# Three small experts of a mixture layer run in the third, fifth and seventh place instead of the second, fourth and sixth

## The reference, cut to what matters

```python
def moe_swiglu(h, w_router, w_gate, w_up, w_down):
    logits = (h @ w_router).astype(jnp.float32)
    top_vals, top_idx = lax.top_k(logits, TOP_K)
    top_w = jax.nn.softmax(top_vals, axis=-1)
    combine = jnp.sum(jax.nn.one_hot(top_idx, N_EXPERTS) * top_w[..., None], axis=-2)
    y = jnp.zeros_like(h)
    for e in range(N_EXPERTS):
        y = y + combine[..., e:e + 1] * swiglu(h, w_gate[e], w_up[e], w_down[e])
    return y
```

## Time and profile before

| | us |
|---|---|
| median of 3 runs | 1440.68 (1440.64 to 1440.73) |
| the profiled execution, own time | 1441.36 |
| its span, first to last instruction | 1439.6 |

### The profile page before, as it was taken

One profiled execution on the slowest core, in us unless ns is written; L12 is line 12 of the kernel. 1 busy time (PEld: TensorE's weight loads), 2 busy tenths in 40 slices (PEclk: granted clock), 3 DMA queues, 4 the chain that ended last, 5 costly groups with the idle time before them and its releaser, 6 DMA issues.

```text
span 1439.6 us, 17466 instructions
## 1 busy us (share of the span) xinstructions
PE 1421.6 (99%) x6728; PEld 1154.7 (80%) x6728; DVE 1169.4 (81%) x1050; ACT 989.4 (69%) x991; POOL 55.4 (4%) x61
## 2 busy tenths in 40 slices
PE   9999999999999999999999999999999999999997
PEld 8977888888887788887778887778887778888885
DVE  5777755556677769889999889999889999899896
ACT  6566553434565668778887778887778877777774
POOL 1000000000000009200000000000000000002000
PEclk9999999999999999999999999999999999999999
DMA  9933655546653369999999999999999999999991
GB/s 350 376 102 120 203 179 201 183 140 197 200 173 125 127 236 370 422 396 371 422 421 421 422 420 393 421 422 420 422 421 395 418 422 421 421 397 375 421 382 56
DMA packets 96489, 460.08 MB, mean 320 GB/s; under 512 B 7656, under 2 KB 13304, under 8 KB 53392
## 3 DMA queue, kind: packets, MB, share of 16 engines
q1 hardware_dynamic: 91632, 444.63, 78.8%
q10 hardware_dynamic: 3312, 9.46, 1.8%
q0 software_dynamic: 1456, 4.79, 0.9%
HBM read 447.85 MB, written 11.01 MB: 319 GB/s over the span
## 4 chain that ended last, share of the span: by engine, by line
PE 83%; DVE 8%; ACT 4%; issue 3%; DMA 2%; SPq 0%; ACTq 0%; DVEq 0%
PE A L498 15%; PE A L500 15%; PE A L499 15%; PE DN L498 5%; PE DN L500 5%; PE DN L499 5%; DVE wlo L472 4%; PE A L504 3%; PE A L505 3%; PE DN L2016 2%; ACT whi L465 2%; DVE wlo_more L472 1%; DMA raw_more<-in_moe_w_down 1%; PE T L2030 1%; PE DN L504 1%
## 5 line engine op out<-in xcount | busy, mean ns | idle before, releaser
L472 DVE TENSOR_TENSOR wlo<-raw,whi 128x2048 fp32r<-128x2048 f32 (+1 forms) x252 | 563.8, 2251 | 124.2 <-ACT whi L465 123.6
L465 ACT ACTIVATE whi<-raw 128x2048 fp32r<-128x2048 f32 (+1 forms) x252 | 472.0, 1885 | 158.9 <-PE A L500 83.3
L472 DVE TENSOR_TENSOR wlo<-raw_more,whi 128x2048 fp32r<-128x2048 f32 x74 | 168.2, 2288 | 11.1 <-ACT whi L465 10.8
L498 PE MATMUL A<-whi,hTh 128*128 128x512 f32 (+2 forms) x448 | 174.4, 389 | 0.8 <-DVE wlo L472 0.7
L499 PE MATMUL A<-wlo,hTh 128*128 128x512 f32 (+2 forms) x448 | 169.9, 379 | 0.0
L500 PE MATMUL A<-whi,hTl 128*128 128x512 f32 (+2 forms) x448 | 169.8, 379 | 0.0
L498 PE MATMUL A<-whi,heTh 128*128 128x512 f32 x420 | 166.5, 396 | 0.0
L500 PE MATMUL A<-whi,heTl 128*128 128x512 f32 x420 | 163.9, 390 | 0.0
L499 PE MATMUL A<-wlo,heTh 128*128 128x512 f32 x420 | 163.6, 390 | 0.0
L465 ACT ACTIVATE whi<-raw_more 128x2048 fp32r<-128x2048 f32 x74 | 140.6, 1916 | 23.1 <-PE A L500 9.6
L472 DVE TENSOR_TENSOR wlo_more<-raw,whi_more 128x2048 fp32r<-128x2048 f32 x57 | 130.4, 2287 | 19.2 <-ACT whi_more L465 19.2
(11 more groups left out here) (367 smaller groups left out, 2314.4 us busy)
## 6 DMA issues: line engine op xcount, KB each, us to landing
raw<-in_moe_w_up SPq DMA_DIRECT2D x79, 1024.0 KB, 11.3
raw<-in_moe_w_down SPq DMA_DIRECT2D x78, 1024.0 KB, 12.7
raw<-in_moe_w_gate SPq DMA_DIRECT2D x77, 1024.0 KB, 12.9
raw_more<-in_moe_w_gate SPq DMA_DIRECT2D x35, 1024.0 KB, 13.5
raw_more<-in_moe_w_down SPq DMA_DIRECT2D x34, 1024.0 KB, 13.5
raw_more<-in_moe_w_up SPq DMA_DIRECT2D x33, 1024.0 KB, 12.5
raw<-in_w_in SPq DMA_DIRECT2D x22, 1024.0 KB, 6.8
raw<-in_dense_w_down SPq DMA_DIRECT2D x11, 1024.0 KB, 4.9
```

Of the source, the lines that this page charges most:

```text
L465: nc.scalar.activation(split_slot(u, e)[0][:, :n], raw_of(u, e)[:, :n], ACT.Copy).then_inc(hi_done, 1)
L472: nc.vector.tensor_tensor(lo[:, :n], raw_of(u, e)[:, :n], hi[:, :n].bitcast(F32), ALU.subtract).then_inc(lo_done, 1)
L498: nc.tensor.matmul(o, hi, wh, start=start, stop=False)
```

## The change

The tuple of small places becomes (2, 4, 6), counted from 0, and the arithmetic that turns an expert's rank by size into its place is adapted: the places are now computed counted from one (1, 2, 4, 6, 8 for the large, 3, 5, 7 for the small), and one is taken off where the scratch rows are computed.

```diff
-SMALL_AT = (1, 3, 5)
+SMALL_AT = (2, 4, 6)
...
+            turns_from_one = cst[:, K_IOTA + 1:K_IOTA + 1 + NE]
...
-            done(nc.vector.scalar_tensor_tensor(turn_raw[:], small[:], -4.5, place_of[:], ALU.mult, ALU.add))
+            done(nc.vector.scalar_tensor_tensor(turn_raw[:], small[:], -3.5, place_of[:], ALU.mult, ALU.add))
...
-            done(nc.vector.tensor_scalar(turn[:], turn_raw[:], 2.0, NE - 1.0, ALU.mult, ALU.min))
+            done(nc.vector.tensor_scalar(turn[:], turn_raw[:], 2.0, 1.0, ALU.mult, ALU.max))
...
-            done(nc.vector.tensor_scalar(turn_row[:], turn[:], float(P), None, ALU.mult))
+            done(nc.vector.tensor_scalar(turn_row[:], turn[:], -1.0, float(P), ALU.add, ALU.mult))
...
-            done(nc.vector.tensor_scalar(is_last[:], turn[:], NE - 1.5, None, ALU.is_gt))
-            done(nc.vector.tensor_scalar(not_last[:], turn[:], NE - 1.5, None, ALU.is_lt))
+            done(nc.vector.tensor_scalar(is_last[:], turn[:], NE - 0.5, None, ALU.is_gt))
+            done(nc.vector.tensor_scalar(not_last[:], turn[:], NE - 0.5, None, ALU.is_lt))
             done(nc.vector.tensor_tensor(taken[:], turn[:].unsqueeze(1).broadcast_to([P, NE, NE]),
-                                         turns.unsqueeze(2).broadcast_to([P, NE, NE]), ALU.is_equal))
+                                         turns_from_one.unsqueeze(2).broadcast_to([P, NE, NE]), ALU.is_equal))
```

## The result

| | before | after |
|---|---|---|
| median of 20 runs, us | 1440.76 (1440.60 to 1442.40) | 1442.83 (1442.15 to 1444.92) |
| ratio to before, 95% interval | | 1.0015 (1.0008 to 1.0021) |
| profiled span, us | 1439.6 | 1442.7 |

The changed kernel is 2.07 us slower: inside the range of 1439.9 to 1446.0 and inside the 0.2% called no change, but three times the 0.7 us of the forecast. The profiled run's own time was 1444.51 us, 1.68 above the median, so its span shows 3.1 us where the medians show 2.1: 0.1 before the experts begin, 0.56 in the first seven places, 2.22 in the eighth up to its last unit and 0.3 behind that.

What follows compares the result with a forecast made beforehand. PE was taken to set the places' times, with DMA also near its limit. Terms 0 + 0 + 0.7 + 0 + 0 = +0.7 us, added to the median 1440.68, gave 1441.4 us, range 1439.9 to 1446.0.

Steps and rivals of the forecast that it cites:

- What bounds the places: All places: PE sets the large ones, PE with DVE the small; PE's 4.6 us of waits bound any gain.
- three signs of being wrong: PE waiting over 3 us in the eighth place, the seventh over 100 us, or a small place below 98 us.
- The boundaries (term 0): First seven places: same large-small boundaries in both orders, so their sum stays unchanged to about 0.1 us.
- The stall at the end of a small place (term 0): Last small place: its extra 0.53 us, read as emptied buffers, stays in the seventh; -0.5 if it goes.
- `weigh_last` (term 0): DVE, seventh place: 1.2 us of work moves into a small place, hidden by 1.45 us of idling; otherwise 1.2.
- The eighth place (term +0.7): Eighth place's start: without stock, gains and gathers cost loads 6.2 us; cushions of 1.4 and 4.1 leave 0.7.
- the step on SP's queue: Eighth place's loads, seven buffers: cost 0, hidden by what is in flight; without that cover 2 to 3 us more.
- the cushion at unit 14: Large place with empty start: DVE finished unit 14 at 1224.27, PE began it at 1228.40, 4.1 us in hand.
- The turns between the DMA queues: Gathers beside loads: equal turns would end the gathers in 10 us, term about 1 us; trace said not to show it.
- The starved eighth place: Eighth place: gathers meet an empty ring and the splits' lead over PE fails, +4.8, 1445.5 us; chance 0.21.
- the stock helps: Small places start fuller, the 0.53 us goes, the eighth place hides its transfers: 1440.2 us; chance 0.14.
- the change is clearly faster: Small places' waits vanish: needs 2.9 of 4.6 us, 1437.1 us with all 3.6 gone; chance 0.03.

Runs made afterwards that it cites:

- e6: The kernel before plus two extra 0.52 MB loads right behind the gains, at the eighth place's start: 1440.89 us, ratio 0.9998.
- e8: The kernel before with the gathers held for 12 splits of the eighth place and the gains for 24: 1440.73 us, ratio 0.9997.
- e9: The changed kernel with nine buffers instead of seven for the eighth place's first six loads, gathers waiting for those six splits: 1442.25 us, ratio 1.0008.
- e10: The changed kernel run once more, unaltered, as yardstick on the same chip: 1443.46 us, ratio 1.0016 to the kernel before.
- e7: e3 with nine buffers instead of seven for the first six loads of the eighth place: 1441.01 us, ratio 1.0002.
- e3: The changed kernel with the gathers held for 12 splits of the eighth place and the gains for 24: 1441.43 us, ratio 1.0004.
- e1: The changed kernel with the final gains' load issued behind the gathers, after 24 splits of the eighth place: 1440.68 us, ratio 1.0002.
- e12: The changed kernel with the gathers held until 8 units of the eighth place are split, gains early as before: 1441.62 us, ratio 1.0008.
- e2: The changed kernel with the gathers held until 12 units of the eighth place are split, gains early: 1441.42 us, ratio 1.0004.
- e11: e9 with the gains issued late, behind the gathers: 1440.94 us, ratio 1.0004.

## Why the prediction was right, and where its size was off

**What bounds the places** was right. The large ones take 118.58 to 118.63 us in the new order too, the large ahead of a large one 118.94, the small ones 98.31 where nothing disturbs them. No version gained on the kernel before beyond its interval, as the 4.6 us of waits had bounded. None of the three signs of being wrong came: PE's wait rows in the eighth place sum to 2.2 us, the seventh took 98.31, and no small place went below 98. But the first of them, set at 3 us of waits, was blunt, since the rows show only half of what a place loses.

**The boundaries (term 0)**: right. The first seven places differ by 0.56 us in the profiles, and 0.51 of it is a stall of 1.04 us in one small place where there was one of 0.53 before.

**The stall at the end of a small place (term 0)**: right in size, but not in its place. I had it in the seventh, where the same row of events ended before, and had read it as buffers that ran empty. It isn't tied to a place. The kernel before has 98.84 in its sixth place in one profile and 98.34 to 98.35 there with the edits of e6 and e8; the new order has 99.35 or 99.43 in the third in two profiles and 98.25 to 98.53 in the other new-order ones. What sets it off in an execution wasn't tried.

**`weigh_last` (term 0)**: right. In its new place it filled the gap that had been 1.45 us, and 0.22 were left:

```profile
1283.77 0.60 DVE L1444 TENSOR_SCALAR cw<-cst,posc,combc 128x128 f32<-128x128 f32 x2
1284.59 2.29 DVE L472 TENSOR_TENSOR wlo_more<-raw_more,whi_more 128x2048 fp32r<-128x2048 f32 x1 [0.22 <-ACT whi_more L465]
```

**The eighth place (term +0.7)**: the mechanism was right, the size wrong. That the total stayed in the range is owed to its upper end, which was there for other cases. The term measured 2.0 to 2.2 us in the three profiles of an empty start with all transfers early (118.69, 118.61, 118.49 against 116.47). Two steps failed.

First, "that cover" in the step on SP's queue. It said seven buffers would still keep the queue fed, cost 0, because a load issued 7 us ahead lands in time. But a queue that just lands its loads isn't a full one: the rate fell to 369 to 384 GB/s for 12 us, and e9 against e10 prices that at 0.6 us, as long as gains and gathers come early; with both late, e7 gained nothing on e3. The step had named 2 to 3 us for this case.

Second, the cushion at unit 14 was read 0.6 us too large. The step counted from the end of DVE's subtraction (1224.27) to PE's start (1228.40), 4.1 us. But PE starts this unit only when DVE has also made `aTl`, the remainder of the activations, and DVE does that behind the subtraction. Before, then after, with PE's start after:

```profile
1224.19 0.68 DVE L1504 TENSOR_TENSOR aTl<-T,aTh 128x512 fp32r<-128x512 f32 x1
```

```profile
1349.35 0.68 DVE L1505 TENSOR_TENSOR aTl<-T,aTh 128x512 fp32r<-128x512 f32 x1
1350.09 0.50 PE L498 MATMUL DN<-whi,aTh 128*128 128x512 f32 x1 [0.18 <-DVE aTl L1505]
```

So before, `aTl` was done at 1224.87, and 3.5 us were in hand. The step's own sum is then 6.2 - 1.4 - 3.5 = 1.3 us instead of 0.7. e9, where the rate has no dip and mainly the bytes count, lost 117.88 - 116.47 = 1.4, and the longest new wait of PE in it is this one:

```profile
1348.31 0.50 PE L498 MATMUL DN<-whi,aTh 128*128 128x512 f32 x1 [0.50 <-DVE aTl L1505]
```

That 0.6 and 1.4 make up the changed kernel's loss is no test, for both are differences over e9; that 1.3 from the rows of before meets the 1.4 is one, though of a single profile.

**The turns between the DMA queues** were misread, in the prediction as an average over too long a window. The Trainium skill (DMA: Bandwidth & Descriptors, "Queues, rings and completion order") has each engine take turns between the queues that have work, by packets. The trace agrees, once one looks only at the time in which both queues move data. For 10 us of it, 1330 to 1340 in the changed kernel (packets, MB, share):

```profile
q1 hardware_dynamic: 388, 2.80, 67.2%
q0 software_dynamic: 391, 1.41, 35.0%
```

The packets that the profile counts are equal in number, but the loads' are on average 7.2 KB and the gathers' 3.6 KB, so that the gathers get a third of the bytes. By this third of 421 GB/s the 2.10 MB take 15 us (an estimate); in the trace their packets run from 1327 to 1343. In the prediction's row of 25 us they were a quarter of the loads only because they were done long before its end. Its estimate of 10 us took equal turns to mean equal bytes, so the 1 us that it gave isn't what the rule says.

**The rivals.** The starved eighth place had been put at +4.8, with the lead of the splits over PE lost and the ring running dry. The ring's part came, with 0.6 us. Of the 4.1 us of lead, 3.5 counted; the other 0.6 went to what that rival had named, a token conversion (DVE's `aTl`) in order behind a late split; less than half of its price was paid. That the stock helps, or that the change is clearly faster, is out. That e1 took away more than theory A allowed fits its later gathers, since a delay alone takes 1.1 to 1.3 us away in e12; it wasn't isolated.

Open: why the medians of e2 and e3 lie 0.7 us above e1's, with eighth places that explain 0.5 and nothing of it, and what starts the 1 us stall in the third place. The intervals don't part these runs. Totals also vary behind the last unit: from its first matmul to the end e10's profile has 1.2 us more than e9's.

## What to carry to other kernels

In a ring where DMA and PE run within about 10% of each other, a transfer costs nothing or nearly its full time depending on what ran before it (here 0 and 2.16 us of 2.5); so order the work such that the part with extra transfers follows the part that fills the buffers. When a step is moved, look at what is in stock where it begins, not at the sum of the loads. A look-ahead that shrinks (nine buffers to seven) where the stock is lowest can cost time: 0.6 us here, and nothing once the extra transfers were moved away. A cushion is read up to the last input that the waiting engine needs, not up to the one that is being followed. And when two queues share the DMA engines, compare their packets and bytes in the stretch where both have work.

## What the runs showed that I had not expected

- POOL's first gather took 4.40 us to issue in e1 and 5.04 in e11, where it was POOL's first transfer for some 738 us; with a plain transfer 17 us ahead of it, 1.12. The long idle time alone doesn't explain it: in e3, e7 and e8 the first gather came after 751 us without a transfer and took 2.35 to 2.37. The cause is open.
- A queue two loads shallower at a hold lowers the rate from 418 to 378 GB/s for 12 us while the DMA engines' busy share still reads 1.00: the share alone doesn't show it, the GB/s do. Nor do the GB/s alone show a loss: the kernel before has 369 in the same 12 us and loses nothing, because it has units in stock.
- While loads and gathers both had work, the DMA engines moved as many packets of the one queue as of the other (388 and 391 in 10 us), so the queue with the larger packets got two thirds of the bytes.
